# The last three gate/value projections as seven block products over half of the tokens

## Chip, core and metric

One Trainium2 chip; the kernel runs on one of its cores. The metric is the device time of one execution in microseconds (us). The kernel before was run three times: 2764.35, 2764.82 and 2764.85 us, median 2764.82.

## What is computed

A two-layer transformer in float32 on 512 tokens of width 1024. Twelve or so matrix stages follow one another: a hybrid attention mixer, memory attention, a convolutional feed-forward network, then SwiGLU networks around a pooling/Hyena mixer and a latent attention (MLA). The change is in the last three SwiGLU networks, `ffn1`, `ffn2` and `ffn3`:

```python
x = x + 0.5 * (silu(h @ w_gate) * (h @ w_up)) @ w_down     # h = rmsnorm(x) * g
# h: (512, 1024), w_gate and w_up: (1024, 2816), w_down: (2816, 1024)
```

## The kernel before

Activations lie transposed: features on the 128 partitions, the 512 tokens along the free axis, `DC` = 8 chunks of 128 features. 2816 hidden features are `FC` = 22 tiles. Weights come from memory in packs of 128 x 1024 floats (512 KB), in the order of `STREAM`: an up pack is all 8 chunks of one gate or one value tile, so that packs 2f and 2f+1 are the gate and the value tile f; a down output takes three packs (8, 8 and 6 chunks).

Each float32 operand is split into a rounded high part and a low part (type fp32r), and each product is three matmuls: high x high, high x low, low x high (`pack`, L823 to L825). Who does what for a pack n:

- SyncE issues the load into `raw[n % 2]` once the low part of pack n-2 is made (L707).
- ScalarE copies it to `whi[n % 4]` (`split_high`, L1545) once TensorE has used pack n-4.
- GpSimd computes `wlo = raw - whi` (`split_low`, L772).
- TensorE does 24 matmuls of 512 columns into a bank of PSUM, one of four in turn.

In the up phase (`project` on TensorE, `feed_forward`, `up_step` on the others) VectorE takes the gate and the value bank, each times `rstd` (L2248), ScalarE applies SiLU (L1663), VectorE multiplies them (L2271), ScalarE makes the high part (L1665), VectorE the low part (L2275), for all 22 tiles. Then the down phase gives 8 outputs in turn. In `residual` and `chunk` VectorE adds each into x (L2176), multiplies by the norm's weight with a tensor_scalar (`gained`, L2147), makes the low part `lin_lo` (L2150) and adds the square to `sumsq` (L2155); ScalarE makes the square (L1560) and the high part (L1565). The root of the mean square isn't needed for the next products, since it scales their result: TensorE sums over partitions (`stats`, L839) after the first pack of the next stage, ScalarE takes the root (L1570), VectorE its reciprocal (L2163) and clears `sumsq` (L2166), and `rstd` multiplies the products when they are taken from PSUM.

The very last output of `ffn3` is computed in two halves of 256 tokens (L1524 to L1526), so that the final norm of one half goes beside the other's matmuls (`last_residual`, `last_sums`).

What sets the order are counting semaphores: each engine runs its own program in order and waits for counts. Loops are `Fori` bodies with counts computed from the loop's register.

## Time and profile before

| | us |
|---|---|
| median of three runs | 2764.82 |
| span of the profiled execution | 2761.3 |
| TensorE matmul busy | 2733.8 (99%) |
| VectorE busy | 1166.5 (42%) |
| GpSimd busy | 1111.9 (40%) |
| ScalarE busy | 1039.8 (38%) |
| `ffn1` | 1459 to 1819 |
| `ffn2` | 1819 to 2179 |
| `ffn3` | 2396 to 2752 |

The profile names TensorE's matmuls PE and its weight loads PEld, VectorE DVE, ScalarE ACT, GpSimd POOL, SyncE SP. Matmuls are pipelined: one lasts 0.39 us in the records while the next starts earlier, so for TensorE the step from start to start counts, not the duration.

### The profile page before, as it was taken

How to read it: one execution, taken by the hardware profiler on the slowest of the kernel's cores; microseconds unless marked ns; L12 is line 12 of the kernel's file. 1: busy time of each engine (PE TensorE's matmuls, PEld its weight loads, DVE VectorE, ACT ScalarE, POOL GpSimd, SP SyncE). 2: the span in 40 equal slices, each digit the busy share in tenths (PEclk: the TensorE clock that was granted, in tenths of full speed). 3: DMA queues.
4: the chain of work that ended last, by engine and by line, in shares of the span. 5: the costliest groups of instructions: out<-in, count | busy, mean ns of one | idle time of the engine just before them, and what ended most of it. 6: DMA issues, size and time to landing. Idle time of an engine off the chain costs nothing.

```text
span 2761.3 us, 35493 instructions
## 1 busy us (share of the span) xinstructions
PE 2733.8 (99%) x12420; PEld 2172.9 (79%) x12420; DVE 1166.5 (42%) x1908; ACT 1039.8 (38%) x1594; POOL 1111.9 (40%) x475
## 2 busy tenths in 40 slices
PE   9999999999999999999999999999999999999999
PEld 7777777888888888857888888888888754888887
DVE  5886534755534224256883222122221366422211
ACT  4555533444333223343233222232222466422222
POOL 3234433444444443523224444544445410444443
PEclk9999999999999999999999999999999999999999
DMA  5333322333333232322113323333333210323332
GB/s 168 121 98 117 106 78 63 92 99 99 99 106 99 91 99 91 114 76 88 54 46 107 99 91 104 106 95 99 99 98 105 87 39 9 107 91 99 98 102 89
DMA packets 80030, 257.29 MB, mean 93 GB/s; under 512 B 11577, under 2 KB 16697, under 8 KB 79691
## 3 DMA queue, kind: packets, MB, share of 16 engines
q1 hardware_dynamic: 73424, 244.74, 28.5%
q10 hardware_dynamic: 6522, 11.43, 1.3%
q8 instruction: 53, 0.87, 0.1%
q14 instruction: 31, 0.25, 0.0%
HBM read 249.98 MB, written 6.03 MB: 93 GB/s over the span
## 4 chain that ended last, share of the span: by engine, by line
PE 88%; issue 7%; POOL 2%; DVE 2%; ACT 1%; DMA 0%; POOLq 0%; DVEq 0%; ACTq 0%
PE ps L823 25%; PE ps L824 25%; PE ps L825 25%; POOL wlo L772 2%; PE ps L1463 1%; PE ps L1432 1%; PE ps L1445 1%; PE ps L1213 1%; PE ps L1242 1%; PE ps L1436 1%; PE ps L1192 1%; PE ps L1261 1%; PE ps L1119 1%; PE ps L1129 1%; PE ps L1052 0%
## 5 line engine op out<-in xcount | busy, mean ns | idle before, releaser
L772 POOL TENSOR_TENSOR wlo<-raw,whi 128x1024 fp32r<-128x1024 f32 x449 | 1098.2, 2449 | 1605.1 <-ACT whi L1545 1580.3
L823 PE MATMUL ps<-lin_hi,whi 128*128 128x512 f32 x2200 | 864.0, 393 | 0.0
L825 PE MATMUL ps<-lin_hi,wlo 128*128 128x512 f32 x2200 | 856.3, 389 | 0.0
L824 PE MATMUL ps<-lin_lo,whi 128*128 128x512 f32 x2200 | 856.1, 389 | 0.0
L1545 ACT ACTIVATE whi<-raw 128x1024 fp32r<-128x1024 f32 x452 | 473.1, 1052 | 517.7 <-PE ps L825 444.7
L823 PEld LDWEIGHTS ps<-lin_hi,whi 128*128 128x128 f32 x2200 | 413.0, 188 | 92.3 <-issue 6.1
L824 PEld LDWEIGHTS ps<-lin_lo,whi 128*128 128x128 f32 x2200 | 413.0, 188 | 88.4 <-issue 3.1
L825 PEld LDWEIGHTS ps<-lin_hi,wlo 128*128 128x128 f32 x2200 | 412.9, 188 | 85.7
L823 PE MATMUL ps<-act_hi,whi 128*128 128x512 f32 x858 | 334.0, 389 | 0.0
L825 PE MATMUL ps<-act_hi,wlo 128*128 128x512 f32 x858 | 333.8, 389 | 0.0
L824 PE MATMUL ps<-act_lo,whi 128*128 128x512 f32 x858 | 333.8, 389 | 0.0
L1665 ACT ACTIVATE act_hi<-hidden 128x512 f32 (+1 forms) x88 | 55.6, 632 | 462.5 <-DVE hidden L2271 462.5
L2248 DVE TENSOR_TENSOR up<-ps,rstd 128x512 f32<-128x512 f32 x88 | 60.8, 691 | 395.4 <-PE ps L825 395.4
L2176 DVE SCALAR_TENSOR_TENSOR x<-ps,x 128x512 f32 x64 | 44.3, 692 | 366.5 <-PE ps L825 361.6
L823 PEld LDWEIGHTS ps<-act_hi,whi 128*128 128x128 f32 x858 | 161.0, 188 | 35.1 <-POOL wlo L772 0.8
L825 PEld LDWEIGHTS ps<-act_hi,wlo 128*128 128x128 f32 x858 | 161.0, 188 | 33.6
L824 PEld LDWEIGHTS ps<-act_lo,whi 128*128 128x128 f32 x858 | 161.0, 188 | 33.1
L2248 DVE TENSOR_TENSOR gate<-ps,rstd 128x512 f32<-128x512 f32 x88 | 60.8, 691 | 189.7 <-PE ps L825 188.9
L1560 ACT ACTIVATE scratch<-x 128x512 f32 x64 | 40.6, 634 | 213.0 <-DVE x L2176 212.9
L2275 DVE TENSOR_TENSOR act_lo<-hidden,act_hi 128x512 f32 x88 | 60.9, 693 | 81.1 <-ACT act_hi L1665 81.1
L823 PE MATMUL ps<-o_hi,whi 128*128 128x512 f32 x240 | 94.0, 392 | 0.0
L824 PE MATMUL ps<-o_lo,whi 128*128 128x512 f32 x240 | 93.4, 389 | 0.0
(420 smaller groups left out, 2769.7 us busy)
## 6 DMA issues: line engine op xcount, KB each, us to landing
raw<-in_packs SPq DMA_DIRECT2D x456, 512.0 KB, 3.5
table<-bias_scratch ACTq DMA_DIRECT2D x12, 256.0 KB, 3.2
bias_scratch<-biasrow ACTq DMA_DIRECT2D x16, 160.0 KB
x<-in_x_t SPq DMA_DIRECT2D x4, 512.0 KB, 8.4
out_t<-x SPq DMA_DIRECT2D x14, 128.0 KB, 1.9
bias_scratch<-biasrow ACTq DMA_DIRECT2D x4, 320.0 KB
mem<-in_mem_t ACTq DMA_DIRECT2D x1, 1024.0 KB, 7.8
pool_count<-in_pool_count ACTq DMA_DIRECT2D x1, 1024.0 KB, 4.8
```

The source lines that it names most:

```text
L772: pool.tensor_tensor(wlo[:, n % 4, :], raw[:, n % 2, :], whi[:, n % 4, :].bitcast(F32), ALU.subtract).then_inc(low_split, 1)
L823: pe.matmul(target, wh, hi[:, k, :], start=(chunk0 + at == 0), stop=False)
L824: pe.matmul(target, wh, lo[:, k, :], start=False, stop=False)
L825: mm = pe.matmul(target, wl, hi[:, k, :], start=False, stop=(chunk0 + at == total - 1))
L1119: mm = pe.matmul(ps[:, att2.banks(u)[0], 0:M], mem_q[:, 2 * h + c, qt * P:(qt + 1) * P], mem_k[:, 2 * h + c, :], start=(c == 0), stop=(c = ...
L1129: mm = pe.matmul(ps[:, 2 + c, :], mem_v[:, j, (2 * h + c) * P:(2 * h + c + 1) * P], mprobs_t[:, h % 2, j, :], start=(j == 0), stop=(j == 1))
L1545: act.activation(whi[:, n % 4, :], raw[:, n % 2, :], ACT.Copy).then_inc(high_split, 1)
L1560: act.activation(squares[:, d % 2, :], x[:, row, :].rearrange("p a t -> p (a t)"), ACT.Square).then_inc(squares_ready, 1)
L1665: act.activation(act_hi[:, bass.ds(f, 1), :].rearrange("p a t -> p (a t)"), h_buf, ACT.Copy).then_inc(hidden_high, 1)
L2176: dve.scalar_tensor_tensor(out=xc, in0=ps[:, j, :], scalar=factor, in1=xc, op0=ALU.mult, op1=ALU.add).then_inc(outs_done, 1)
L2248: dve.tensor_tensor(target, ps[:, 2 * g + side, :], rstd[:, :], ALU.mult).then_inc(outs_done, 1)
L2275: dve.tensor_tensor(low, h_buf, high, ALU.subtract).then_inc(hidden_low, 1)
```

## The change

**Seven products.** For each of the 22 tiles of `ffn1`, `ffn2` and `ffn3` the gate and the value pack are taken as a 2 x 2 block matrix (gate or value tile, first or second half of the 1024 input features), and the activations as a 2 x 2 block matrix (first or second half of the features, first or second 256 tokens). The product is formed by seven block products and sums (Winograd's form of Strassen's algorithm) in place of eight. A block product is 4 chunks x 3 matmuls of 256 columns.

- Activations: `fold` makes, for each pair of chunks (c, c+4), seven blocks of 256 tokens: the four blocks and three sums of them, high and low part each (`folds[c]`). Outputs before such a stage come in the order 0, 4, 1, 5, ... (`BY_PAIRS`).
- Weights: two load instructions bring both packs into `raw_pair[p % 2]`. VectorE makes four sums (`pair_sum`), two in SBUF and two in PSUM banks 6 and 7; ScalarE makes high parts in four slots of `whi` (`split_direct`, slot 2 with 1024 columns, the others 512) and of the two PSUM sums (`split_sum`); GpSimd makes low parts of the slots, VectorE those of the PSUM sums (`sum_low_part`).
- Products: pair p uses banks 0 to 2 or 3 to 5. Products 1, 3, 5 and 7 (k = 0, 2, 4, 6) go to the same bank, the last three on top of what is there, and before each of them ScalarE copies the bank out (`copy_term`). VectorE adds the quarters (`quarter`, of 256 columns for k = 0, 1, 3), multiplies by `rstd` (k = 2, 4) and forms the hidden product in PSUM (`make_hidden`, `low_hidden`).
- Groups: only 8 hidden tiles fit beside that, so up and down alternate in groups of 6, 8 and 8 tiles (`GROUPS`), and x is added to after each group's down phase; the first two down outputs of a group begin without its last tile (`down_pair`).
- The root and reciprocal now come inside the first pair of a stage (after product 4).
- The last output's halves have 8 chunks in place of 22.

**Around it.** Semaphores used once are merged with others, the plain packs' loads are written out, buffers of the MLA stage lie in another order.

The core of the diff:

```diff
+GROUPS, FIRST_TILE, DOWN_PACK, GROUP_AT = (6, 8, 8), (16, 0, 8), (2, 0, 1), (0, 6, 14)
+BY_PAIRS = (0, 4, 1, 5, 2, 6, 3, 7)
+PRODUCTS = (          # (weight slot, half of the slot, bank, fold, begins)
+    (0, 0, 0, 0, True), (0, 1, 2, 3, True), (1, 1, 0, 5, False), (1, 0, 1, 1, True),
+    (2, 0, 0, 4, False), (2, 1, 2, 2, False), (3, 0, 0, 6, False),
+)
+BY_WEIGHT = (0, 3, 5, 6)
...
+        def seven_pair(name, g, p, i, s=None, outs=None):        # TensorE
+            def product(k, steps):
+                slot, half, bank, fold, begins = PRODUCTS[k]
+                for c in steps:
+                    if s is not None:
+                        pe.wait_ge(chunk_ready, CHUNK_BASE[s] + 4 * c + (1, 2, 2, 3, 3, 4, 4)[fold])
+                    at = half * T + c * P
+                    wh, wl = whi[:, slot, at:at + P], wlo[:, slot, at:at + P]
+                    target = ps[:, banks[bank], 0:T // 2]
+                    pe.matmul(target, wh, folds[c][:, fold, 0, :], start=begins and c == 0, stop=False, skip_group_check=True)
+                    pe.matmul(target, wh, folds[c][:, fold, 1, :], start=False, stop=False, skip_group_check=True)
+                    mm = pe.matmul(target, wl, folds[c][:, fold, 0, :], start=False, stop=c == 3, skip_group_check=True)
+                return mm
...
+            if s is not None:
+                for first in range(3):
+                    for early in (0, 1, 3):
+                        if first == 0:
+                            weights_and_bank(early)
+                        product(early, (first,))
+            for k in range(7):
+                early = s is not None and k in (0, 1, 3)
+                if not early:
+                    weights_and_bank(k)
+                if k in (2, 4, 6):
+                    pe.wait_ge(terms_copied, value(i, 8, 4 * pair + (1, 3, 4)[k // 2 - 1]))
+                product(k, (3,) if early else range(4)).then_inc(packs_used if k in BY_WEIGHT else product_made, 1)
+                if k == 3 and s is not None:
+                    stats(s, FOLD_STAT)
...
+        def down_pair(name, g):                                   # TensorE
+            phase, chunks = f"{name}_down{g}", GROUPS[g]
+            pe.wait_ge(hidden_low, hidden_before(name, g) + chunks - 1)
+            for cut in (range(chunks - 1), (chunks - 1,)):
+                for j in range(2):
...
+        def seven_window(name, g, p, i, n, s=None, next_packs=None):     # ScalarE
+            split_direct(name, g, p, 3, i)
+            if p:
+                silu(name, g, p - 1, i, n)
+            copy_term(name, g, p, i, 0)
...
+            ahead(0)
+            if p:
+                hidden_split(name, g, p - 1, i, n)
+            copy_term(name, g, p, i, 1)
+            if next_packs is None:
+                split_sum(name, g, p + 1, 0, i)
+            copy_term(name, g, p, i, 2)
+            if next_packs is None:
+                split_sum(name, g, p + 1, 1, i)
+            if s is not None:
+                root(s, FOLD_STAT)
+                copy_term(name, g, p, i, 3)
+                ahead(1)
+            else:
+                ahead(1)
+                copy_term(name, g, p, i, 3)
+            ahead(2)
...
+        def fold(s, j):                                           # VectorE
+            c, side, d = j // 2, j % 2, BY_PAIRS[j]
+            dve.tensor_scalar(gained[:, side, :], x[:, d, :], cols[:, at:at + 1], None, ALU.mult).then_inc(gain_applied, 1)
...
+            if side == 0:
+                order(dve.tensor_tensor(gated[:, FIRST_HALF], b12, b11, ALU.subtract))
+                fold_low_part(s, c, 0)
+            else:
+                dve.tensor_tensor(gated[:, LAST_HALF], b22, b12, ALU.subtract).then_inc(fold_made, 1)
+                order(dve.tensor_tensor(upped[:, FIRST_HALF], b22, gated[:, FIRST_HALF], ALU.subtract))
+                dve.tensor_tensor(upped[:, LAST_HALF], b21, upped[:, FIRST_HALF], ALU.subtract).then_inc(fold_made, 1)
+                for k in range(1, 4):
+                    fold_low_part(s, c, k)
...
+        def residual_to_pairs(phase, s, factor, name):            # VectorE
+            for j in range(DC):
+                take(phase, j, BY_PAIRS[j], factor)
+                fold(s, j)
+                first_pair(name, 0, j - 4)
...
+        def seven_window(name, g, p, i, n, more=True, s=None):    # VectorE
+            if p:
+                quarter(name, g, p - 1, i, 3)
+                quarter(name, g, p - 1, i, 4)
+            if more:
+                pair_sum(name, g, p + 1, i, 0)
+            if p:
+                make_hidden(name, g, p - 1, i, n)
+            if more:
+                pair_sum(name, g, p + 1, i, 1)
+            if p:
+                low_hidden(name, g, p - 1, i, n)
+            if more:
+                pair_sum(name, g, p + 1, i, 2)
+                sum_low_part(name, g, p + 1, i, 0)
+            quarter(name, g, p, i, 0)
+            if more:
+                pair_sum(name, g, p + 1, i, 3)
+                sum_low_part(name, g, p + 1, i, 1)
+            if s is not None:
+                norm(s)
+            quarter(name, g, p, i, 1)
+            quarter(name, g, p, i, 2)
```

## Rows read from the trace of the kernel before

**Rows 1.** The page's busy line: busy us, share of the span, instructions.
```profile
PE 2733.8 (99%) x12420; PEld 2172.9 (79%) x12420; DVE 1166.5 (42%) x1908; ACT 1039.8 (38%) x1594; POOL 1111.9 (40%) x475
```
**Rows 2.** Windows view, PE in ffn1: stretch, length, busy (instructions), clock, DMA share, GB/s.
```profile
1459.00:1818.50 359.50, 359.50 (x1585) 1.00 0.32 100
```
**Rows 3.** Timeline, PE, down phase: start, duration, engine, line, operation, shape.
```profile
2722.00 0.39 PE L823 MATMUL ps<-act_hi,whi 128*128 128x512 f32 x1
2722.23 0.39 PE L824 MATMUL ps<-act_lo,whi 128*128 128x512 f32 x1
```
**Rows 4.** Groups by line, ACT, 1459 to 2180: busy, mean ns, idle and releaser.
```profile
L1545 ACT ACTIVATE whi<-raw 128x1024 fp32r<-128x1024 f32 x137 | 144.5, 1055 | 202.3 <-PE ps L825 202.1 <-issue 0.2
L1665 ACT ACTIVATE act_hi<-hidden 128x512 f32 (+1 forms) x44 | 27.8, 632 | 232.7 <-DVE hidden L2271 232.7
L1663 ACT ACTIVATE gate<-gate 128x512 f32<-128x512 f32 x44 | 27.0, 614 | 5.8 <-DVE gate L2248 5.8
```
**Rows 5.** Timeline, PE, first half of the last output.
```profile
2735.95 0.28 PE L1524 MATMUL ps<-act_hi,whi 128*128 128x256 f32 x1
...
2743.39 0.28 PE L1526 MATMUL ps<-act_hi,wlo 128*128 128x256 f32 x1
```
**Rows 6.** Lines L1048 and L1061, PE's sequencer, 236 to 239: ns, first and last start.
```profile
L1048 PEldq EVENT_SEMAPHORE  x1: 51/51/51, 236.7 to 236.7; - x1
...
L1061 PEldq EVENT_SEMAPHORE  x1: 51/51/51, 238.2 to 238.2; - x1
```
**Rows 7.** Groups by line and timeline: other widths, and VectorE back to back.
```profile
L772 POOL TENSOR_TENSOR wlo<-raw,whi 128x1024 fp32r<-128x1024 f32 x449 | 1098.2, 2449 | 1605.1 <-ACT whi L1545 1580.3 <-DVE sumsq L2327 24.0
L789 POOL TENSOR_TENSOR wlo<-raw,whi 128x512 fp32r<-128x512 f32 x4 | 5.4, 1352 | 19.5 <-ACT whi L2061 19.4
...
1825.15 0.69 DVE L2248 TENSOR_TENSOR gate<-ps,rstd 128x512 f32<-128x512 f32 x1 [0.58 <-DVE sumsq L2166]
1825.76 0.68 DVE L2248 TENSOR_TENSOR up<-ps,rstd 128x512 f32<-128x512 f32 x1
...
2756.27 0.38 ACT L1620 ACTIVATE rstd<-ps 128x256 f32<-128x256 f32 x1 [1.94 <-PE ps L1533]
...
raw<-in_packs SPq DMA_DIRECT2D x456, 512.0 KB, 3.5
```
**Rows 8.** Timeline, PE and DVE, the two halves of the last output.
```profile
2743.72 0.42 DVE L2194 SCALAR_TENSOR_TENSOR x<-ps,x 128x256 f32<-128x256 f32 x1 [5.83 <-PE ps L1526]
2747.97 1.75 DVE L2198 RECIPROCAL rstd<-rstd 128x256 f32<-128x256 f32 x1 [3.83 <-ACT rstd L1616]
2749.75 2.77 DVE L2200 TENSOR_TENSOR x<-x,rstd 128x256 f32<-128x256 f32 x8
...
2752.17 0.28 PE L1526 MATMUL ps<-act_hi,wlo 128*128 128x256 f32 x1
...
2752.49 0.42 DVE L2194 SCALAR_TENSOR_TENSOR x<-ps,x 128x256 f32<-128x256 f32 x1
```
**Rows 9.** Timeline, gains before ffn1 with GpSimd, and one before ffn2.
```profile
1437.68 2.66 POOL L772 TENSOR_TENSOR wlo<-raw,whi 128x1024 fp32r<-128x1024 f32 x1 [2.05 <-ACT whi L1545]
...
1424.66 1.80 DVE L2147 TENSOR_SCALAR scratch<-x,cols 128x512 f32 x1 [0.15 <-DVE x L2176]
...
1438.83 1.79 DVE L2147 TENSOR_SCALAR scratch<-x,cols 128x512 f32 x1
...
1769.62 0.49 DVE L2147 TENSOR_SCALAR scratch<-x,cols 128x512 f32 x1 [0.15 <-DVE x L2176]
```
**Rows 10.** Timeline and windows view, PE, around the one stretch of lower clock.
```profile
223.36 0.52 PE L1066 MATMUL ps<-ident,pair_probs 128*128 128x128 f32 x2 [1.98 <-DVE pair_probs L2477]
...
224.00:227.50 3.50, 3.50 (x15) 0.51 0.22 41
```
**Rows 11.** Timeline, root and reciprocal at the start of ffn2.
```profile
1816.70 1.28 ACT L1570 ACT_TABLE_LOAD   x1
1819.84 0.69 ACT L1570 ACTIVATE rstd<-ps,small 128x512 f32<-128x512 f32 x1 [1.85 <-PE ps L839]
...
1820.56 3.35 DVE L2163 RECIPROCAL rstd<-rstd 128x512 f32<-128x512 f32 x1 [3.39 <-ACT rstd L1570]
1824.08 0.48 DVE L2166 MEMSET sumsq<- 128x512 f32 x1 [0.17 <-DVE rstd L2163]
```

More of the change, by code:

```diff
@@ new lines, in seven @@
+        def seven(name, after, last_order):
+            for g, pairs in enumerate(GROUPS):
+                base, down = PACK_BASE[f"{name}_up{g}"], PACK_BASE[f"{name}_down{g}"]
+                with sp.Fori(0, pairs // 2 - 1) as i:
+                    for p in (2, 3):
+                        load_pair(name, g, p, i, value(i, 8, base + 4 * (p - 1)))
+                order = last_order if g == 2 else range(DC)
+                for d in range(DC):
+                    load_plain(down + d, base if d < 2 else down + d - 1, DRAM_BASE[f"{name}_down"] + 3 * order[d] + DOWN_PACK[g])
+                    if d == 1 and (g < 2 or after):
+                        for p in range(2):
+                            load_pair(name if g < 2 else after, g + 1 if g < 2 else 0, p, None, base + 4 * (pairs - 1 + p))
@@ L780, in _ @@
             split_low(n, None)
-        with pool.Fori(1, times) as i:
-            for n in range(4):
-                split_low(n, i)
-        for n in range(queries - rest, queries):
-            split_low(n, None)
+        split_packs(4, PACK_BASE["ffn1_up0"] - 4)
+        seven("ffn1")
+        seven("ffn2")
+        split_packs(PACK_BASE["mla_down"], queries - PACK_BASE["mla_down"])
         for n in range(queries, queries + 4):
@@ L1333, in query_sums, with seven @@
+        def seven(name, s, before):
+            for g in range(3):
+                seven_up(name, g, s, before)
+                seven_down(name, g)
+        seven("ffn1", 5, "pool_hyena_out")
+        seven("ffn2", 6, "ffn1_down2")
         def query_sums():
@@ new lines, in seven @@
+        def seven(n, name, s, after):
+            for g, pairs in enumerate(GROUPS):
+                seven_window(name, g, 0, None, n, s=s if g == 0 else None)
+                with dve.Fori(0, pairs // 2 - 1) as i:
+                    for p in (1, 2):
+                        seven_window(name, g, p, i, n)
+                last = pairs - 1
+                seven_window(name, g, last, None, n, more=False)
+                quarter(name, g, last, None, 3)
+                quarter(name, g, last, None, 4)
+                make_hidden(name, g, last, None, n)
+                low_hidden(name, g, last, None, n)
+                phase = f"{name}_down{g}"
+                if g == 2 and after is None:
+                    last_residual(phase, s + 1, factor=0.5)
+                elif g == 2 and after not in SEVENS:
+                    residual(phase, s + 1, factor=0.5)
+                elif g == 2:
+                    residual_to_pairs(phase, s + 1, 0.5, after)
+                else:
+                    for j in range(DC):
+                        take(phase, j, j, 0.5)
+                        first_pair(name, g + 1, j - 4)
```

511 lines of the change are left out of this document (397 added, 114 removed).

## The prediction

> **What bounds the kernel now.** I read the page's busy line first: TensorE (PE) is busy 99% of the span, every other engine 38 to 42% [rows 1]. A pipelined PE is also "busy" with gaps between issues, so the next view is the windows over the three stages that the change rewrites. It shows 1585 matmuls of 512 columns in 359.5 us [rows 2], 0.2268 us each, which is the step between two neighbours in the timeline (2722.00 to 2722.23) [rows 3]. No matmul waits there: from 1459 us on the stage is a solid row of matmuls, and its time is their number times 0.2267 us (528 for 22 pairs of packs and the same kind for the down projection). The other engines wait for PE: the groups view gives ScalarE 202.1 us of idle before its high halves, put down to PE [rows 4]. So what shortens PE's stream shortens the kernel, until the work of another engine takes longer than PE's.
>
> **The products.** A pair of up packs (gate and value tile) costs PE 2 x 8 x 3 = 48 matmuls of 512 columns, 48 x 0.2267 = 10.88 us. Seven products of 4 x 3 matmuls over 256 columns are 84 matmuls. Their step has to be read, because half the columns need not take half the time. The last output of the kernel is already computed with 256 columns: between 2735.95 and 2743.39 lie 62 steps, 0.120 us each [rows 5]. Half of 0.2267 would be 0.1133, so 0.0067 us is the price of a weight load for each half-width matmul. 84 x 0.120 = 10.08 us. The gain is 0.80 us a pair and 66 x 0.80 = 52.8 us for the 66 pairs of three stages.
>
> Does PE's sequencer keep up when each product brings waits? In the memory projection it passed from the wait of L1048 (236.7) to that of L1061 (238.2), with 24 pairs of weight load and matmul between them, in 1.5 us: at most 0.0625 us a pair of instructions [rows 6]. 84 such pairs take at most 5.3 us of 10.08, so some ten waits with register values a pair of packs are hidden. The Trainium skill ("TensorE: Matmul & The Clock Gate", Back-to-back issue gap) would give 262 cycles, 109 ns, for 256 columns and 518 cycles, 216 ns, for 512. By it the pair falls from 10.36 to 9.17 us and the stages gain 79 us. The rows show 0.120 and 0.2267, and I go by them; the page's value is a rival below.
>
> **The helpers inside a pair.** Each has to fit 10.08 us, at the durations of [rows 4, 7].
> - VectorE: four sums and two low parts of weights, two scalings, hidden and its low part: 10 operations of 512 columns at 0.69 us, and three of 256 at 0.42: 8.2 us (before: four at 0.69, 2.8 us). Back to back it takes 0.61 and 0.35 [rows 7, 8], so 7.2 us plus hand-overs of 0.15.
> - ScalarE: three halves of 512 at 0.63, one of 1024 at 1.05, two sums at 0.63, four copies of product tiles of 256 at 0.38 to 0.42, SiLU 0.61, hidden 0.63: 7.1 us.
> - GpSimd: three of 512 at 1.35 and one of 1024 at 2.45: 6.5 us.
> - DMA: 1 MB a pair, 3.5 us to land for 512 KB, so 7 us if the two never overlap.
> All fit, but PE now waits three times a pair (before products 3, 5 and 7) for a copy that ScalarE makes of the bank it adds to. Cover is one product, 12 x 0.120 = 1.44 us. The copy starts about 0.2 us after the product's last column (2752.17 to 2752.49 for start of matmul and its reader [rows 8]), takes 0.42 and reaches PE 0.1 later: 0.7 us of slack. What is queued ahead of it on ScalarE ends in time: before copy 1 the high half of slot 3 (0.63) and SiLU (0.61), 1.5 of 1.64 us; before copy 3 a chain VectorE, ScalarE of hidden product, high part and weight sum that I end at 4.5 of 4.52 us after the pair began. I take nothing lost; bounds are 0 and, if each of the three misses by 0.3 us, 0.9 us a pair. VectorE ends its window 1.2 us before the product it then waits for. Its last step (scaling) gates the next SiLU, which has 0.6 us to spare.
>
> **From norm to first product.** Before, the last chunk's gain, high and low part hid behind seven chunks of the first pack. Now products 1, 2 and 4 run over three chunk pairs first: 27 x 0.120 = 3.24 us, with the fourth of product 1 3.6. The last fold costs VectorE, from the output's end: 0.2 to its start, residual add 0.69 and hand-over 0.15, gain 0.49, three differences of 256 columns with hand-overs 1.4, and the two low parts that product 2 waits for 1.4: about 4.4 us. That alone leaves 0.8 us idle. But VectorE comes late to it. An even chunk costs it 3.1 us, an odd one 4.8, the three steps of the next stage's weight sums 1.25 each, while outputs come every 5.44 us (24 x 0.2267); I put the last take 0.3 us late. And a tensor_scalar can't finish while GpSimd is in a tensor_tensor: at 1438.83 it took 1.79 us and ended 0.3 after GpSimd's row did, at 1769.62, with GpSimd idle, 0.49 [rows 9]. GpSimd's 2.45 us for weight slot 2 now falls on the last gain, 1.6 to 2 us more than at rest. Idle: 2 us before ffn2 and ffn3. Before ffn1 outputs 1 and 2 end together, and in the rows of before VectorE works without a pause with a 1.8 us gain each time [rows 9]; with folds added I get a take 3.3 us late and 5 us idle. Sum 9 us; bounds 2.5 (0.8 each) and 15. A long idle has a second price: after 1.98 us without a matmul at 221 to 223 us, in a stretch of small ones, the granted clock was 0.51 from 224 to 227.5 (1.2 of 2.4 GHz) [rows 10]. I add 1.7 us for one such stretch.
>
> **The root inside the first pair.** Before, root, reciprocal (3.35) and memset (0.48) took 4.7 us, the table load (1.28) stood ahead of them, and only VectorE's takes waited, with four banks between them and PE [rows 11]. Now ScalarE's queue has SiLU of pair 1 ahead of copy 1 of pair 2, and that SiLU needs the reciprocal. From the end of the sums: root at 2.6 (it stands behind a weight sum and the table load), reciprocal to 6.1, memset to 6.7, takes to 8.0, SiLU 8.7, copy 9.1. PE reaches product 3 of pair 2 at 7.4. Idle 1.7 us, with small ones after it 2.2; three times, 6.5 us. Bounds 3 and 9.
>
> **Groups.** Down projections are cut into 6, 8 and 8 chunks with the same 528 matmuls. The second up group's first weights are summed under the previous outputs; down's first two outputs start with all chunks but the last (5 x 2 x 0.68 = 6.8 us), which covers the 3.5 us of the last hidden. I take nothing for six such borders, 0 to 2 us each as bound.
>
> **The end.** Before, half of the last output (66 x 0.120 = 7.9 us) ran beside the first half's norm, and VectorE took the second half at 2752.49, when both were just done: 8.8 us after the first take (2743.72) [rows 8]. Now the second half takes 24 x 0.120 = 2.9 us, but the norm chain (sums, root, reciprocal 1.75, eight products 2.77) is as long as ever, so the take still comes 8.8 us after the first. What was beside it now stands ahead: 504 x 0.2267 + 24 x 0.120 = 117.1 against 462 x 0.2267 + 66 x 0.120 = 112.7 us. That loses 4.5 us, and PE, idle some 6 us by then, does its last small matmuls at the lower clock: 5.5 us in all, bounds 4.4 and 6.5. Renamed semaphores and the other order of address regions cost nothing: no step is added, and the operations' sizes stay.
>
> **Sum.** Span 2761.3 - 52.8 + 9 + 1.7 + 6.5 + 5.5 = 2731.2. The median of the runs is 3.5 us above the profiled span, so 2734.7, say 2735 us. Its own bounds: 2764.8 - 52.8 + 2.5 + 3 + 4.4 = 2722 and 2764.8 - 52.8 + 16.7 + 9 + 6.5 = 2744.
>
> **Rivals.**
> - Borders and partial misses: the six borders lose 2 us each, or one copy gate a pair misses by up to 0.4 us. For: ScalarE's chain to copy 3 has 0.7 us in all, and in the last pair of a group 1024-wide high halves stand in it. Against: that is the only dense stretch. 2744 to 2761 us, 0.22.
> - ScalarE's queue becomes the bound (slower): hand-overs with two register waits cost 0.1 to 0.2 us more than I charge, the hidden chain ends after product 3, and copies 2 and 3 are late in every pair. It decides from 0.46 us a pair (30.1 / 66) on, the point at which nothing is gained; at 0.9 us 2735 + 59 = 2794. For: three engines hand over eight times in 10 us. Against: 7.1 of 10.08 us busy, 0.7 us slack at each gate. 2768 to 2795, 0.13.
> - Seven products aren't shorter: if the 256-column step were 0.130 us when weights alternate between slots, 84 x 0.130 = 10.9 us and only the costs are left, 2788. Nothing in [rows 5] hints at it, where high and low weights alternate too: 0.02.
> - The page's gap holds: 79 instead of 52.8 us, by a step of 0.109 in place of 0.120. The same mechanism in rows: the step falls to half of 0.2267, 0.1133, gaining 90 - 52.8 = 37 more at most, 2698 to 2720. Against: the 62 steps of 0.120. With costs at their lower bounds as another way there: 0.08.
>
> **Chances.** Forecast 0.55, borders 0.22, rival queue 0.13, no shorter 0.02, below 0.08. Faster by over 0.2% (5.5 us, about what a measurement of this kernel tells from no change) 0.83, within 0.03, slower 0.14. The range leaves out half of the lower case and the two slower ones: 2716 to 2764.
>
> **What would show it.** In the timeline of the changed kernel: steps of 0.120 us and pairs 10.08 apart; PE idle only before ffn1, ffn2, ffn3 (5, 2, 2 us) and in each stage's second pair (2 us, put down to ScalarE's copies); the last gain before each stage over 1.5 us; VectorE's takes of the last output's halves 8.8 us apart. PE idle before products 3, 5 or 7 of inner pairs would make it wrong, as would a step other than 0.120.

## The result, and the profile of the changed kernel

The kernel became slower: 2795.73 us median (2793.96 to 2796.25, 4 runs) against 2764.59 (2763.43 to 2764.85), a ratio of 1.0112 with a 95% interval of 1.0098 to 1.0126. The forecast was 2735 us, in a range of 2716 to 2764. Even its range does not hold the result.

The page's busy line shows at once which engine got the work: VectorE went from 42% to 62%, PE from 99% [rows 1] to 97%.
```profile
PE 2701.7 (97%) x14754; PEld 2250.7 (81%) x14754; DVE 1735.8 (62%) x2622; ACT 1271.1 (45%) x2155; POOL 1240.7 (44%) x607
```
The windows view cuts three stretches out: ffn1's second up group (8 pairs), the down phase behind it, and ffn1's first up group (6 pairs, with the stage's entry in it).
```profile
1564.20:1651.20 87.00, 82.14 (x673) 80.91 (x672) 73.92 (x95) 48.10 (x91) 55.51 (x32) 1.00 0.33 115
1651.20:1694.80 43.60, 43.60 (x195) 36.09 (x194) 12.35 (x17) 10.67 (x13) 19.33 (x9) 1.00 0.20 62
1454.60:1531.50 76.90, 65.21 (x507) 63.12 (x506) 65.30 (x85) 44.74 (x78) 41.98 (x25) 0.93 0.33 109
```
The columns are length, then busy time and instructions of PE, weight loads, VectorE, ScalarE and GpSimd, and the granted clock. The down phase is as dense as before, 43.6 us for 192 matmuls. Eight pairs are 672 matmuls, 80.6 us at 0.120 us, and take 87.0. Six pairs are 60.5 us and take 76.9. So there are two losses: one inside the pairs, 6.4 us in each of the six groups of eight, and one in the first group of each stage (76.9, 75.6 and 72.3 us in ffn1, ffn2, ffn3). ffn1's first product starts at 1454.62 here; in the kernel before its first matmul starts at 1453.39, and the 1459 in the table of the kernel before is the end of its first pack.

**An inner pair.** The timeline of PE around a hole, then VectorE, ScalarE and GpSimd in the same 4 us (start, duration, and in brackets the idle time and what ended it):
```profile
1591.11 0.28 PE L1458 MATMUL ps<-fold,wlo 128*128 128x256 f32 x1
1592.19 0.39 PE L1456 MATMUL ps<-fold,whi 128*128 128x256 f32 x1 [0.81 <-ACT scratch L1956]
...
1585.76 2.31 DVE L2620 TENSOR_TENSOR ps<-scratch 128x256 f32<-128x256 f32 x1 [0.28 <-PE ps L1458]
1588.10 0.70 DVE L2623 TENSOR_TENSOR ps<-ps,rstd 128x512 f32<-128x512 f32 x1
1588.71 1.06 DVE L2540 TENSOR_TENSOR ps<-raw_pair_odd 128x512 f32<-128x512 f32 x1
1589.68 0.68 DVE L2629 TENSOR_TENSOR ps<-gated,ps 128x512 f32<-128x512 f32 x1
...
1590.51 0.60 ACT L1964 ACTIVATE ffn_hi<-ps 128x512 f32 x1 [2.49 <-DVE ps L2629]
1591.00 0.38 ACT L1956 ACTIVATE scratch<-ps 128x256 f32<-128x256 f32 x1
1591.26 0.60 ACT L1821 ACTIVATE whi<-ps 128x512 fp32r<-128x512 f32 x1
1591.74 0.40 ACT L1956 ACTIVATE scratch<-ps 128x256 f32<-128x256 f32 x1
...
1596.51 3.85 POOL L884 TENSOR_TENSOR wlo<-raw_pair_odd,whi 128x1024 fp32r<-128x1024 f32 x2 [1.32 <-ACT whi L1811]
1596.91 2.31 DVE L2620 TENSOR_TENSOR ps<-scratch 128x256 f32<-128x256 f32 x1 [0.29 <-PE ps L1458]
```
Read it backwards. ("Term copy" is ScalarE's copy of a product out of the bank that the next product adds to, "quarter" a sum that VectorE makes of such terms, "hidden split" the high part of the hidden product; "loop pairs" below are those inside a group's loop, that is all but its first and its last.) PE's fifth product waits for the third term copy (1591.74). ScalarE works in order: that copy stands behind the hidden split (1590.51), the second copy and a weight sum. The hidden split had idled 2.49 us for make_hidden (VectorE, 1589.68), and this stands behind quarter 3 (L2620), which took 2.31 us for 256 columns. The last two lines, one pair later, show why: GpSimd's 1024-wide low part (the first of two in its row) had begun 0.4 us before. Quarter 3 adds two operands that both lie in SBUF; quarters 0 and 1, with one of two in PSUM, take 0.42 and 0.43 us. The groups view of VectorE over the whole span has it in every pair:
```profile
L2620 DVE TENSOR_TENSOR ps<-scratch 128x256 f32<-128x256 f32 x66 | 132.1, 2001 | 17.4 <-PE ps L1458 17.4
L2540 DVE TENSOR_TENSOR ps<-raw_pair_even 128x512 f32<-128x512 f32 x33 | 40.9, 1240 | 0.2
L2540 DVE TENSOR_TENSOR ps<-ps,raw_pair_even 128x512 f32<-128x512 f32 x33 | 22.6, 686 | 0.2
```
The first weight sum, two SBUF operands, takes 1.24 us; the third, with one operand in PSUM, 0.69 us.

**The entry of ffn1.** PE, ScalarE, VectorE and GpSimd between the last down product and the second pair:
```profile
1464.04 0.58 PE L1456 MATMUL ps<-fold,whi 128*128 128x256 f32 x1 [5.58 <-DVE fold L2565]
1467.51 0.55 PE L1456 MATMUL ps<-fold,whi 128*128 128x256 f32 x1 [2.46 <-issue]
1480.55 0.39 PE L1456 MATMUL ps<-fold,whi 128*128 128x256 f32 x1 [1.06 <-ACT scratch L1956]
...
1462.82 3.64 ACTq L2380 DMA_DIRECT2D rope<-in_rope  x8
1466.51 0.63 ACT L1811 ACTIVATE whi<-raw_pair_even 128x512 fp32r<-128x512 f32 x1 [3.06 <-issue]
1476.36 1.28 ACT L1811 ACT_TABLE_LOAD   x1
1478.30 1.28 ACT L1960 ACT_TABLE_LOAD   x1
...
1458.25 0.68 DVE L2591 SCALAR_TENSOR_TENSOR x<-ps,x 128x512 f32<-128x512 f32 x1
1458.96 2.56 DVE L2573 TENSOR_SCALAR scratch<-x,cols 128x512 f32<-128x512 f32 x1
...
1458.90 2.34 POOL L884 TENSOR_TENSOR wlo<-raw_pair_even,whi 128x1024 fp32r<-128x1024 f32 x1 [3.64 <-ACT whi L1811]
```
The first hole holds the late last take (1458.25; the outputs ended at 1454.6) and the gain beside GpSimd. The second is ScalarE issuing eight rope transfers, 3.64 us, ahead of a weight split and a copy that PE needs. The third has two table loads in front of SiLU; e7 and e9 show that the wait for the reciprocal makes this hole and the loads do not.

### The profile page after: what moved, and what is told of

Its sections match the earlier page's. It is cut to its first block, busy times and chain, and to the rows that moved or that the text cites. A ratio compares the mean times of both kernels' runs of the same rounds, so it can differ in the third digit from the quotient of the medians.

```text
span 2794.4 us, 42283 instructions
## 1 busy us (share of the span) xinstructions
PE 2701.7 (97%) x14754; PEld 2250.7 (81%) x14754; DVE 1735.8 (62%) x2622; ACT 1271.1 (45%) x2155; POOL 1240.7 (44%) x607
## 4 chain that ended last, share of the span: by engine, by line
PE 64%; issue 16%; DVE 9%; POOL 7%; ACT 3%; DMA 0%; ACTq 0%; POOLq 0%; DVEq 0%
PE ps L935 13%; PE ps L936 13%; PE ps L937 13%; POOL wlo L884 4%; POOL wlo L866 3%; PE ps L1456 3%; PE ps L1458 3%; PE ps L1457 3%; DVE ps L2620 2%; DVE ps L2540 1%; PE ps L1673 1%; PE ps L1642 1%; PE ps L1655 1%; PE ps L1325 1%; DVE scratch L2573 1%
## 5 line engine op out<-in xcount | busy, mean ns | idle before, releaser
L866 POOL TENSOR_TENSOR wlo<-raw,whi 128x1024 fp32r<-128x1024 f32 x317 | 781.3, 2470 | 1133.1 <-ACT whi L1752 1108.5
L1456 PE MATMUL ps<-fold,whi 128*128 128x256 f32 x1848 | 531.5, 288 | 59.8 <-ACT scratch L1956 41.5
L1457 PE MATMUL ps<-fold,whi 128*128 128x256 f32 x1848 | 524.3, 284 | 0.0
L1458 PE MATMUL ps<-fold,wlo 128*128 128x256 f32 x1848 | 524.3, 284 | 0.0
L935 PE MATMUL ps<-lin_hi,whi 128*128 128x512 f32 x1144 | 452.0, 395 | 0.0
L937 PE MATMUL ps<-lin_hi,wlo 128*128 128x512 f32 x1144 | 445.4, 389 | 0.0
L936 PE MATMUL ps<-lin_lo,whi 128*128 128x512 f32 x1144 | 445.3, 389 | 0.0
L1456 PEld LDWEIGHTS ps<-fold,whi 128*128 128x128 f32 x1848 | 355.8, 193 | 73.5 <-ACT scratch L1956 51.6
L1457 PEld LDWEIGHTS ps<-fold,whi 128*128 128x128 f32 x1848 | 356.2, 193 | 0.9 <-issue 0.5
L1458 PEld LDWEIGHTS ps<-fold,wlo 128*128 128x128 f32 x1848 | 356.0, 193 | 0.0
L884 POOL TENSOR_TENSOR wlo<-raw_pair_even,whi 128x512 fp32r<-128x512 f32 (+1 forms) x132 | 222.9, 1698 | 222.4 <-ACT whi L1811 222.4
L884 POOL TENSOR_TENSOR wlo<-raw_pair_odd,whi 128x512 fp32r<-128x512 f32 (+1 forms) x132 | 224.6, 1714 | 147.7 <-ACT whi L1811 147.7
L2620 DVE TENSOR_TENSOR ps<-scratch 128x256 f32<-128x256 f32 x66 | 132.1, 2001 | 17.4 <-PE ps L1458 17.4
```

What stands on the lines that cost most here:

```text
L866: pool.tensor_tensor(wlo[:, n % 4, :], raw[:, n % 2, :], whi[:, n % 4, :].bitcast(F32), ALU.subtract).then_inc(low_split, 1)
L884: pool.tensor_tensor(wlo[:, slot, 0:width], slot_source(p, slot), whi[:, slot, 0:width].bitcast(F32), ALU.subtract).then_inc(low_split, 1)
L935: pe.matmul(target, wh, hi[:, k, :], start=(chunk0 + at == 0), stop=False)
L936: pe.matmul(target, wh, lo[:, k, :], start=False, stop=False)
L937: mm = pe.matmul(target, wl, hi[:, k, :], start=False, stop=(chunk0 + at == total - 1))
L1456: pe.matmul(target, wh, folds[c][:, fold, 0, :], start=begins and c == 0, stop=False, skip_group_check=True)
```

## The experiments

Each kernel ran four times, beside seven runs of the kernel before (medians 2763.3 to 2763.9). The length of a group is the time from its first matmul to the first of the next phase. Hole sizes in the text are from start to start of two matmuls (0.12 us where there is none).

Where runs differ by a few us, the lengths of the groups say more than the medians, for one difference lies ahead of the change. In the profiled executions of the change, e7 and e10 ffn1's first product starts at 1454.6 to 1454.9 us, in the ten other changed kernels at 1452.8 to 1453.5. The three have a stretch of half clock (1.2 of 2.4 GHz) at 284 to 288 us, in a dense row of 256-column matmuls, and the hundred matmuls from 283 us on take 15.7 us there against 14.2 in the others; those have their stretch at 223 to 228 us, where it costs nothing that can be seen, or none (e8, e9). PE idles the same ahead of both places in all of them (from start to start 2.35 us at 221 us and 2.0 at 281 us), so what puts the stretch there stays open. It is 1.5 us that belong to no edit.

### Where the inner pairs lose it

**e1_q3_psum: quarter 3 on a PSUM operand.**
```
-  act.activation(terms[p % 2][:, k, :], ps[:, bank, FIRST_HALF], ACT.Copy).then_inc(terms_copied, 1)
+  target = ps[:, bank, LAST_HALF] if k == 3 else terms[p % 2][:, k, :]
+  act.activation(target, ps[:, bank, FIRST_HALF], ACT.Copy).then_inc(terms_copied, 1)
...
-  ins = dve.tensor_tensor(both[:, LAST_HALF], u3, m5, ALU.add)
+  ins = dve.tensor_tensor(both[:, LAST_HALF], both[:, LAST_HALF], m5, ALU.add)
```


> One change: the fourth term copy of each pair (u3) goes into the free second half of its own PSUM bank and not to SBUF, so that quarter 3 adds a PSUM and an SBUF operand and no longer two SBUF operands. Theory A (quarter 3 loses 1.6 us in every pair because VectorE, with two SBUF operands, waits for GpSimd's low part of slot 2; that delay carries through make_hidden and the hidden split into the third term copy and so into PE's fifth product): quarter 3 takes 0.43 us and not 2.00, the 1.07 us hole of the inner pairs goes, 66 pairs x about 1.0 us, 2725 to 2745 us. Rival B (the hole is the length of ScalarE's own queue between two products, whatever VectorE does): quarter 3 shorter, hole stays, 2785 to 2800 us. Rival C (the wait for GpSimd is only handed on to the next operation with two SBUF operands, the first pair sum, which stands before make_hidden): quarter 3 0.43 us, pair sum 0 up from 1.06 to about 2.3 us, hole smaller by 0.4 us at most, 2765 to 2790 us.

2748.6 us (ratio 0.9943, 0.9927 to 0.996). The groups view of VectorE:
```profile
L2621 DVE TENSOR_TENSOR ps<-ps,scratch 128x256 f32<-128x256 f32 x66 | 28.5, 432 | 17.5 <-PE ps L1458 17.5
L2541 DVE TENSOR_TENSOR ps<-raw_pair_even 128x512 f32<-128x512 f32 x33 | 50.8, 1538 | 0.2
L2541 DVE TENSOR_TENSOR ps<-raw_pair_odd 128x512 f32<-128x512 f32 x33 | 47.9, 1452 | 0.2
```
Quarter 3 takes 0.43 instead of 2.00 us. Part of the wait is handed on, as rival C said: pair sum 0 grew from 1.24 and 1.13 to 1.54 and 1.45 us. But 0.3 us handed on against 1.57 us gone is enough. Every group of eight now takes 80.63 us, without a hole; 47 us came back (46.2 of them in the nine groups). Theory A's 2725 to 2745 was missed by 3.6 us: it charged the hole to all 66 pairs, but only the 48 inside the loops have it.

**e2_low_narrow: GpSimd almost taken away.**
```
-  pool.tensor_tensor(wlo[:, slot, 0:width], slot_source(p, slot), whi[:, slot, 0:width].bitcast(F32),
+  pool.tensor_tensor(wlo[:, slot, 0:32], slot_source(p, slot)[:, 0:32], whi[:, slot, 0:32].bitcast(F32),
                      ALU.subtract).then_inc(low_split, 1)
```


> GpSimd's low parts of the weight pairs in the three stages are made of 32 columns instead of 512 or 1024, so almost no GpSimd work lies beside the pairs (the low parts of the weights are left out of the result in these stages; all waits stay). Theory A (GpSimd against VectorE's operations with two SBUF operands): quarter 3 0.43 us, pair sums 0 and 1 about 0.68 us, no hole in the inner pairs; the entries of the stages keep most of their idle time, since there GpSimd works on down packs: 2715 to 2735 us. Rival B (length of ScalarE's queue): the hole stays above 0.7 us, over 2775 us. Rival D (the waits in front of products, each against a register's value, cost PE the 1.07 us by themselves): no change, 2790 to 2800 us.

2734.87 us (0.9895, 0.9878 to 0.9911), 61 us less than with the change. VectorE's instructions were not touched, and the same ones are short:
```profile
L2620 DVE TENSOR_TENSOR ps<-scratch 128x256 f32<-128x256 f32 x66 | 28.6, 433 | 17.5 <-PE ps L1458 17.5
L2540 DVE TENSOR_TENSOR ps<-raw_pair_even 128x512 f32<-128x512 f32 x33 | 23.5, 712 | 0.2
```
This shows the cause: the 1.57 us of quarter 3 and the 0.53 us of the weight sum exist only beside GpSimd's low parts. Rivals B and D fall with it. ScalarE had the same instructions in the same order and all waits stayed; its inner pairs have no hole. Theory A had expected 2715 to 2735 and gets the upper end, because the entries lose more than it knew (below). The other 14 us of the 61 lie in the three first groups (13.7 us shorter than in e1).

**e3_order: the meeting stays, but nothing stands behind it.** On ScalarE hidden_split(p - 1) goes from ahead of copy_term 1 to behind copy_term 2; on VectorE low_hidden goes behind pair_sum 2 and sum_low_part 0.

> Only the order of two queues: on ScalarE the hidden split of the pair before goes behind the third term copy, on VectorE its low part goes behind pair sum 2 and the first sum's low part. All instructions and GpSimd's work stay. Theory A: quarter 3 still takes 2.0 us and more, but nothing that PE waits for stands behind it; PE's hole in the inner pairs falls from 1.07 to at most 0.3 us (VectorE is busy 10.1 us of a pair and PE needs 10.08, so VectorE may become the bound by a little): 2730 to 2750 us. Rival B (length of ScalarE's queue as such): the hole falls by the 0.6 us of one copy, about 2755 us. Rival D (hand-overs in front of products): 2790 to 2800 us.

2748.49 us (0.9945, 0.9928 to 0.9961). The groups view of VectorE over the span:
```profile
L2620 DVE TENSOR_TENSOR ps<-scratch 128x256 f32<-128x256 f32 x66 | 132.7, 2010 | 7.0 <-PE ps L1458 6.4 <-issue 0.5
```
and the windows view of the second up group:
```profile
1560.20:1640.80 80.60, 80.60 (x673) 80.59 (x672) 72.89 (x95) 48.10 (x91) 55.61 (x32) 1.00 0.36 124
```
Quarter 3 is as slow as in the change, VectorE is busy 72.9 of 80.6 us, and PE has no hole. So two things had to come together: an instruction that waits for GpSimd, and a copy queued behind its result. Removing either brings back the same 47 us (46.2 in the nine groups, by either). (VectorE's instructions cost 10.4 us in one pair here, 1580.65 to 1591.05, and 9.1 us on average over the group; it does not become the bound.)

### What the entries lose

With the inner holes gone (e3_order) the first groups still take 74.7, 72.8 and 69.5 us for 60.5 us of products.

**e4_rope: the eight rope transfers.** They move from between the residual and seven(2, ...) into the down phase of ffn1's second group, two for each of four weight splits; the rest is the change.

> Only ScalarE's eight rope transfers are moved, from between the pool and hyena residual and ffn1's first window into the down phase of ffn1's second group, two ahead of each of four weight splits. Theory E (they hold ScalarE's queue for 3.6 us at ffn1's entry and make PE's second hole of 2.87 us there; the clock's fall is not theirs): that hole falls below 0.8 us, nothing is lost in the down phase, 2791 to 2794 us. Rival F (the copy that PE waits for is late for another reason, the last gain and fold on VectorE): hole stays above 2 us, no change within 0.5 us. Rival G: the shorter wait also ends the half clock earlier, and up to 4 us more are gained: 2787 to 2791 us.

2791.98 us (1.01, 1.0083 to 1.0117), 3.75 us less than the change. Only 2.3 us of it lie in ffn1's first group (74.67 against 76.92 us); ffn1 was also reached 1.3 us earlier, which the edit cannot do. The PE hole of 2.46 us ended by "issue" is gone from the trace, and the half clock at ffn1's entry lasts 6.8 instead of 10.2 us. Theory E is right, and a little of G. In the kernel before, the same transfers stood at the same place (4.08 us from 1455.30 on) and PE's row has no hole beside them: the next thing on ScalarE's queue, a high half, had to wait for PE itself.

**e5_gain: gains on ScalarE.** The gain, the multiplication by the norm's weight, is on VectorE in the kernel before too (L2147), so this edit undoes nothing that the change did. ScalarE waited for VectorE's gain there and now waits for the fold of the chunk pair before.
```
-  dve.tensor_scalar(gained[:, side, :], x[:, d, :], cols[:, at:at + 1], None, ALU.mult).then_inc(gain_applied, 1)
+  act.activation(gained[:, side, :], x[:, d, :], ACT.Copy, scale=cols[:, at:at + 1]).then_inc(gain_applied, 1)
```


> The part 'norm weights on VectorE' is undone: the 24 gains of the folded stages run on ScalarE (a copy with a scale, 0.63 us) ahead of the square, and VectorE waits for them. In the kernel with the change the last gain of each entry stands beside a GpSimd low part and takes 2.56 us between PE's last down product and its next one. Theory A (that wait is on the path): PE's entry hole falls from 5.86 to about 4.0 us (3.0 to 1.2 in ffn3), three entries, 5 to 7 us: 2788 to 2791 us. Rival C (handed on: the next operations with two SBUF operands, 0.42 us each, meet the same GpSimd instruction): hole 5.0 to 5.9 us, 2793 to 2796 us. Rival H (ScalarE's longer queue delays the fold's high parts or the weight splits of the down phase): slower than 2797 us. The holes of the inner pairs stay as they are by all.

2790.82 us (1.0099, 1.0083 to 1.0116), 4.9 us less than the change, 4.0 of it in the first groups (1.2, 2.0 and 0.8 us). VectorE at ffn1's entry:
```profile
1456.45 1.77 DVE L2582 TENSOR_TENSOR gated<-scratch 128x256 f32<-128x256 f32 x1 [0.86 <-ACT scratch L1841]
1458.15 0.41 DVE L2583 TENSOR_TENSOR upped<-scratch,gated 128x256 f32<-128x256 f32 x1
```
Both A and C are half right. The 2.56 us gain is gone and PE's first hole fell from 5.86 to 3.97 us (4.28 in ffn2, 2.25 in ffn3). But the next instruction with two SBUF operands meets the same GpSimd row and takes 1.77 instead of 0.42 us.

**e6_four_edits** combines e1, e3, e4 and e5.

> Four edits together: quarter 3 on a PSUM operand, hidden split behind the third term copy, rope transfers moved, gains on ScalarE. If the causes are separate and add up: inner holes gone once and not twice (47 us, since the first two edits each remove the same hole), rope 3.8 us, gains 5 to 7 us: 2736 to 2741 us. If the gains bring nothing (rival C of the run before): 2744 us. If the stages' first group hides one entry delay behind another: 2741 to 2744 us.

2742.27 us (0.9924, 0.9908 to 0.9941): 6.2 us under e3_order, where 3.75 and 4.9 would add up to 8.7. The inner holes went once, as expected. By the groups the entry edits do not overlap: the first groups are 4.9, 2.0 and 0.8 us shorter than in e3_order, 7.7 in all, where e4 and e5 had 2.3 and 4.0 there. What is missing from 8.7 is less than the 1.5 us of clock that each of the two comparisons with the change's profiled execution contains. The forecast of 2736 to 2741 was too hopeful by 1.3 us.

**e7_silu_table** adds one instruction at the end of a stage's first window:
```
+  if s is not None:
+      act.activation(small[:, 92:93], eps_c, ACT.Silu)
```


> As the four edits, and one more instruction: a Silu of one column at the end of each folded stage's first window, so that the loop over pairs is entered with Silu's table loaded. In the kernel with the change the first group's loop loads two tables (1.28 us each) in each of its two turns, the other groups' loops none. Theory I (the loads come from entering the loop with Sqrt's table; they make the PE holes of 1.33 and 1.27 us in the first group): 3 of 4 loads go in each stage, both holes fall below 0.5 us, 3 x 2.2 us = 5 to 8 us less than the four edits alone. Rival J (the loads stay, since each turn chooses a table for Copy anyway): five loads, up to 1 us slower than the four edits.

2738.95 us (0.9909, 0.9893 to 0.9926). In the change each stage's first group had four table loads, two in each turn of the loop over pairs (1476.36, 1478.30, 1498.8 and 1500.8 us in ffn1). Here ffn1's first group has one, ahead of the loop:
```profile
1471.49 1.28 ACT L2003 ACT_TABLE_LOAD   x1
1472.79 0.20 ACT L2003 ACTIVATE small<-small 128x1 f32<-128x1 f32 x1
```
The first groups are 1.24, 1.23 and 1.22 us shorter, 3.7 us in sum. The hole at the loads of the second turn (1.27 us) is gone, but the one in the second pair (1.44 to 1.59 us) stayed: theory I was right on the loads and wrong on that hole. The median gained 3.3 us, although this profiled execution came to ffn1 1.7 us later than that of e6 (1454.84 against 1453.15), with its half clock near 285 and not 225 us.

The Trainium skill ("ScalarE activation tables: per-element evaluation and per-set limits", Table sets in the compiler and the runtime) says that the compiler places table loads block by block; the traces agree: a loop entered with another table than it ends with loads anew in each turn, one entered with the same never.

**e8_late_slot2** also puts the first pair's 1024-wide split behind the last fold on ScalarE, so that GpSimd's long low part comes later.

> As the run before, and the split of the first pair's slot 2 (1024 columns, whose low part holds GpSimd for 2.4 us at the entry) goes behind the last chunk's fold on ScalarE. Theory A (GpSimd's low part meets the fold's two-SBUF operations on VectorE at the entry): all operations of the last fold take 0.42 and 0.68 us, PE's entry hole falls by another 1 to 1.5 us, 2 to 4 us in all; the low part comes in time for product 5, which starts 2.9 us after the fold's last part. Rival K (the low part then comes too late): a new hole of 1 to 2 us in front of product 5, and the sum is within 1 us of the run before, or slower.

2736.06 us (0.9903, 0.9886 to 0.992). The entry holes, from start to start of a matmul, are 2.6 + 1.0, 3.0 + 1.0 and 0.9 + 1.0 us (3.97, 4.28 and 2.25 with e5's gains). But the long low part now meets the second pair's weight sum:
```profile
2375.27 2.89 DVE L2549 TENSOR_TENSOR ps<-raw_pair_odd 128x512 f32<-128x512 f32 x1
2378.07 1.75 DVE L2549 TENSOR_TENSOR raw_pair_odd<-raw_pair_odd 128x512 f32<-128x512 f32 x1
...
2374.72 4.54 POOL L884 TENSOR_TENSOR wlo<-raw_pair_even,whi 128x1024 fp32r<-128x1024 f32 x2 [7.05 <-ACT whi L1811]
```
and in ffn3 a new hole of 1.44 us (2381.99) gives much of it back, so the groups are shorter by only 0.42, 0.39 and 0.46 us. The rest of the 2.9 us between the medians is again the time of reaching ffn1. Moving GpSimd's work moves the meeting; the truth lies between A and K.

**e9_silu_behind: SiLU behind the first term copy.** On ScalarE silu(p - 1) goes behind copy_term 0.

> As the kernel with six edits (late slot 2), and the Silu of the pair before goes behind the first term copy of each pair on ScalarE. There, in each stage's second pair, Silu waits for VectorE's 3.35 us reciprocal, and the first term copy, for which PE's third product waits, stands behind it (PE's hole of 1.6 us). Theory L (that order makes the hole): it falls below 0.3 us, 3 x 1.3 us = 3.5 to 4.5 us: 2731.5 to 2733 us, inner pairs without holes. Rival M (Silu half a copy later makes VectorE's make_hidden late in every inner pair, with VectorE's 0.9 us of slack used up): 0.1 to 0.3 us in each of 63 pairs, 2738 to 2750 us.

2732.64 us (0.9887, 0.987 to 0.9903): 1.1% faster than the kernel before, the fastest of all that keep the whole computation. The hole of the second pair (1.78, 1.31 and 1.59 us in the three stages of e8) is 0.55 us in ffn1 and below 0.4 in the others. The groups are 1.22 to 1.24 us shorter, and the eights stay at 80.63: theory L, though the gain of 3.4 us is just under its 3.5 to 4.5 and the holes (0.55, 0.34 and 0.35 us) stay above its 0.3. So this hole was SiLU waiting for the 3.35 us reciprocal with a copy behind it, and not the table loads.

**e10_copies_first: the third term copy ahead of the weight sum's split.**

> As the run before, and the third term copy goes ahead of the first weight sum's split on ScalarE. In the first pair of a stage that split waits for a pair sum on VectorE that takes 1.8 to 2.9 us beside GpSimd's low parts, and the copy stands behind it (PE's hole of 1.44 us in ffn3, none above 1 us in ffn1 and ffn2 there). Theory L: 1 to 3 us less than the run before, 2729 to 2732 us. Rival N (the weight sum comes later instead, and the next pair's second product waits for its low part): a hole at that place in each pair, slower than the run before.

2735.33 us (0.9897, 0.9881 to 0.9913), 2.7 us more than e9, 1.1 of it in the groups: theory L falls. Rival N's hole does not show either, the eights stay at 80.63. In ffn3's first pair the hole of 1.45 us became one of 2.45. PE now comes earlier to its seventh product, and there waits for a copy that stands behind the root's table load, which begins 11.2 us after the group's start in both kernels:
```profile
2380.22 1.28 ACT L1777 ACT_TABLE_LOAD   x1
2381.52 0.69 ACT L1777 ACTIVATE rstd<-ps,small 128x512 f32<-128x512 f32 x1
2382.11 0.38 ACT L1961 ACTIVATE ps<-ps 128x256 f32<-128x256 f32 x1
```
Behind the longer hole a stretch of lower clock (2383.4 to 2386.8) costs 1.4 us more, so ffn3's group is 1.2 us longer. The other 1.6 us lie ahead of ffn1 (1454.90 against 1453.29), in the half clock at 284 us.

**e11_narrow_again** is e10 with GpSimd's narrow low parts.

> As the run before, with GpSimd's low parts of the weight pairs made of 32 columns only (they are left out of the result). It prices what is left of the meeting of GpSimd and VectorE once no order of a queue passes it on. Theory A: inner pairs are free of holes with and without it, so only the entries gain: 3 to 8 us less than the run before. Rival O (no cost is left): within 1.5 us. On the kernel with the change alone the same edit gave 61 us.

2726.0 us (0.9864, 0.9847 to 0.988): 9.3 us less than e10, of which about 1.4 is that difference ahead of ffn1 and 7.7 lie in the first groups: theory A, by the groups within its 3 to 8. What cost 61 us costs under 10 once no queue passes it on.

**e12_two_sbuf_back** is e10 with quarter 3 on two SBUF operands again.

> As the run with the copies first, but quarter 3 reads its two operands from SBUF again, as in the change. Theory A (the meeting costs only where a copy that PE waits for stands behind it): quarter 3 takes 2.0 us again and the time stays within 1.5 us. Rival P (VectorE, busy 10.1 us of a pair of 10.08 us again, becomes the bound): 0.1 to 0.3 us in each pair, 5 to 20 us more.

2734.54 us (0.9894, 0.9878 to 0.9911), 0.8 us from e10. In its groups view:
```profile
L2627 DVE TENSOR_TENSOR ps<-scratch 128x256 f32<-128x256 f32 x66 | 132.3, 2004 | 5.3 <-PE ps L1458 4.8 <-issue 0.5
```
66 instructions lose 1.57 us each, and the groups of eight still take 80.63 us: theory A, not P. One pair each in the first groups of ffn2 and ffn3 has a new hole of 1.24 us; the three first groups together are 0.6 us longer than in e10, and ffn1 was reached 1.6 us earlier.

## Why the prediction was wrong

**Right.** The 256-column step is 0.120 us in the products too; groups without holes take 80.63 us for 672 matmuls, so the 52.8 us of products are there, and the rival of a shorter step falls. That the 0.0067 us above half of the 512-column step are the price of a weight load no run here shows. Borders and down phases cost nothing: 43.55 us for 192 matmuls. The end was forecast at 5.5 us and measures 5.4: 4.4 by the arithmetic, and 9.8 instead of 8.8 us from the last half's take (2784.58, answering to 2752.49 in [rows 8]) to the end. The takes of the two halves are 8.73 us apart, as forecast.

**The step that failed is the cost of VectorE's helpers, "10 operations of 512 columns at 0.69 us, and three of 256 at 0.42".** Ten of the thirteen have an operand in PSUM and measured 0.67 to 0.70 us (512 columns) and 0.42 to 0.43 (256). Three have both in SBUF, and beside GpSimd they measured 2.00 (quarter 3), 1.24 and 1.13 (pair sum 0), and 1.25 and 1.10 us (pair sum 1): 2.5 us more a pair. I knew that an instruction can wait for GpSimd, but took it for a property of tensor_scalar [rows 9]. The trace of before held the counter-example, for L2155 hidden behind a mean of 0.72 us, for L2158 open in a mean of 2.34. Its line view by minimum, median and maximum has, for VectorE's two-SBUF sums in the residuals:
```profile
L2155 DVE TENSOR_TENSOR sumsq<-sumsq,scratch x64: 681/684/2883, 317.6 to 2393.8; 128x512 f32<-128x512 f32 x64
L2158 DVE TENSOR_TENSOR gained_sq<-gained_sq,gained_squares x8: 678/2888/2893, 743.7 to 842.6; 128x512 f32<-128x512 f32 x8
```
and its timeline shows one such sum beside GpSimd's low part:
```profile
753.00 2.89 DVE L2158 TENSOR_TENSOR gained_sq<-gained_sq,gained_squares 128x512 f32<-128x512 f32 x1
...
752.68 2.66 POOL L772 TENSOR_TENSOR wlo<-raw,whi 128x1024 fp32r<-128x1024 f32 x1 [2.06 <-ACT whi L1545]
```
The Trainium skill ("SBUF — State Buffer", Who interferes with whom) states it: a VectorE instruction with two SBUF inputs contends with a GpSimd instruction that reads SBUF, since its second input comes through a read interface that the two share, and the lock on it is exclusive; with at most one SBUF input it does not contend, unless it runs in one of VectorE's two-port modes, which tensor_scalar can enter. The traces agree: e1_q3_psum and e2_low_narrow give 0.43 instead of 2.00 us, and the sum at 753.00 ends 0.55 us after GpSimd's row (755.34). The gain, a tensor_scalar with one SBUF tensor, waits too (2.56 against 0.49 us); that it runs in such a mode no run here shows.

**How 1.6 us became 1.07 a pair.** The prediction ended the chain "hidden product, high part and weight sum" at 4.5 of 4.52 us and took "nothing lost", with 0 to 0.9 us a pair as bounds. With quarter 3 at 2.31 us the copy is late in each of the 48 loop pairs. That is the forecast's own rival (ScalarE's queue becomes the bound, slower, from 0.46 us a pair on), with its place right and its cause wrong: not hand-overs (e2 has them all) but port meetings. It measured 46.2 us, 0.96 us a loop pair (the nine groups against those of e3_order: 38.4 in the six of eight, 7.9 in the three first); I gave it 0.13. A chain with 0.02 us of slack should not have been booked at nothing.

**The entries and roots** were put at 17.2 us (9 + 1.7 + 6.5) and measure 34.2 in e3_order: 13.8, 11.8 and 8.6, each the first group's length less 60.5 us of products and 0.45 us for the two matmuls of the sums, so holes and lower clock together.
- The rope transfers (2.3 us in ffn1's first group by e4) were not priced at all, though they stand on ScalarE's queue between the residual and the first window.
- ffn2's last take was forecast 0.3 us late and came at 1829.29, 4.0 us after the last output ended (1825.33). I had charged the pile-up of outputs 1 and 2, which end together, to ffn1 alone (3.3 us forecast, 3.6 measured). ffn1's last down phase ends them together too, and VectorE works without a pause from 1795 us on. ffn3, fed by evenly spaced outputs, was 0.65 us late.
- The last gain before each stage took 2.56, 2.56 and 2.63 us, as forecast; taking the gains off VectorE gave back 4.0 us of the first groups by e5, where the forecast had 1.6 to 2 us an entry.
- The lower clock costs 3.3 us in e3_order (1.9 + 1.4), not 1.7, as there are two such stretches.
- The root in the first two pairs was put at 6.5. Its mechanism was right, as e9 shows, but the three table loads that a loop entered with Sqrt's table repeats were not in it: in e3_order the holes in the first groups' second pairs sum to 4.1 us, those at the loads in their fourth pairs to 3.5.

**The sum.** Forecast span 2731.2; plus 46.2 for the loop pairs, plus 17.0 for entries and roots, less 0.1 at the end is 2794.3, against 2794.4 measured. That it closes so well is partly luck: the half clock at 284 us is 1.5 us in no term, and the gap of 0.41 us that each stage of the kernel before had after its first pack (at 1459.29, 1819.23 and 2396.51), 1.2 us in all, stands in none either.

**What stays open.** In the best kernel (e9) the first groups still lose 6.0, 7.0 and 4.9 us, and e11 shows that some 8 us of such a loss (in e10) are GpSimd's. What puts the half clock at 284 us in some executions and at 224 us or nowhere in others is not known. e3_order moved instructions in two queues at once; which of the two moves was needed was not tried apart.

## What to carry to other kernels

Before moving work to VectorE, list for each instruction how many operands lie in SBUF and which GpSimd rows run beside it, and list every tensor_scalar too, since the gains waited with a single SBUF tensor; look at the maximum, not the mean, of such instructions, and keep one operand in PSUM where that is free. In a queue that works in order, put what another engine waits for ahead of what itself waits; here two moved calls, one on each queue, were worth 47 us, as much as removing the slow instruction. A stall that two causes need together is cured by removing the cheaper one, so price the chain and not the instruction.

## What the hardware did that I had not expected

- VectorE's tensor_tensor of 256 columns took 2.31 us beside GpSimd with two SBUF operands (2.00 on average) and 0.43 with one, and the wait is handed on to the next such instruction (1.54 instead of 1.24 us in e1, 1.77 instead of 0.42 in e5).
- A VectorE instruction with a PSUM operand ran undisturbed inside a GpSimd row. From the change's trace, the take of 0.68 us and the gain behind it, which waits:
```profile
1811.88 0.68 DVE L2591 SCALAR_TENSOR_TENSOR x<-ps,x 128x512 f32<-128x512 f32 x1
1812.59 1.91 DVE L2573 TENSOR_SCALAR scratch<-x,cols 128x512 f32<-128x512 f32 x1
...
1811.25 2.97 POOL L866 TENSOR_TENSOR wlo<-raw,whi 128x1024 fp32r<-128x1024 f32 x1 [3.24 <-ACT whi L1752]
```
- A loop entered with another activation table than its body ends with loaded two tables, 1.28 us each, in each turn (four loads in two turns in the change, none inside the loop in e7).
- A stretch of half clock of 3.4 us cost 1.5 us in a dense row of matmuls (at 284 us in the change, e7 and e10) and nothing that can be seen in a sparse one (at 224 us in the others).
